# An RWKV-7 head stage reordered: four closing products of y on GpSimd, its per-head scales on ScalarE, a and b turned ahead of r and k

## The chip, the cores and the metric

One core of one Trainium2 chip runs the whole program. The metric is the device time of one execution in microseconds (us), smaller is better. The engines are named as in the profile: PE (TensorE), DVE (VectorE), ACT (ScalarE), POOL (GpSimd) and SP (SyncE, which here only issues transfers).

## What is computed

Two layers over 512 tokens of width 1024, each a token mixer and a feed-forward part with a normalisation behind either. Layer 0 mixes by a gated MLP, layer 1 by RWKV-7. The change lies in RWKV-7's part that works head by head (16 heads of 64):

```python
kk = (k * k_k); kk = kk / maximum(sqrt(sum(kk * kk, per head)), 1e-12)
k = k * (1.0 + (a - 1.0) * k_a)
# per token: sa = -S kk;  S = S * decay + sa b^T + v k^T;  y = S r      with b = kk * a
y = (y - mean) * rsqrt(var + GN_EPS) * gn_g + gn_b        # mean and var per head
bonus = sum(r * k * r_k, per head) * v
out = ((y + bonus) * g) @ w_o
```

## The kernel before

The dense products (projections, feed-forward, output) stream weight slabs of 512 KB and fill most of the span. Between the last projection and the output product `rw_out` lies the head stage. It has eight steps: step i is token block i // 2 (128 tokens) and half i % 2 of the heads (8 heads, 512 columns). The recurrence over 128 tokens is not run token by token: PE forms the interactions of the decayed vectors a, b, k, r (`gram`), the triangular system is inverted from blocks of 8 up to 64 (`grown`, `inverse`), and products then give y and the new state.

A loop of eight iterations carries several steps at once, written out by hand for every engine: in iteration q the engines prepare step n = q + 1, invert step q, run the products of step s = q - 1 (state, x, u, y) and close step `before` = q - 2. Each engine works in the order in which its code stands. There is no scheduler; semaphores alone tie the engines together. What each does in an iteration, in order:

- DVE: `spread_rows` (rows of the small blocks), the variance of y of `before`, kk and its norm, `decay_before`, `invert_blocks` (14 short dependent operations), the normalising of kk, `scale_b` and `decay_ab` (the vectors b and a), `grow` 0, `decay_kr` (k and r), `sum_bonus`, `grow` 1, `centre_y`, `pass_state` and last `mask_grams`, eight copies of the interactions out of PSUM under a mask, L1222.
- POOL: two masks (`level_of`), four products that scale k (`scale_k`, L478 to L483), two that form r * k * r_k (`bonus_terms`, L492, L495), six that close y (`finish`, L513 to L520), and four copies (`place_diagonal`, L466). All of these but the masks and copies are 128x512.
- ACT: copies out of PSUM, squares, square roots and exponentials; `copy_left` carries the left factor of each level of the inversion (L809), `copy_ub` (L804) the lower half of u.
- PE: `x_product` (L1635, L1638; it waits for the sixth masked copy of the step after), `log_decays` (L1540, L1542), `replicate` (L1580), `u_top`, `y_known`, `x_carry` (L1658), then the levels of the inversion (L1588) with `u_bottom`, `state_change` and `y_rest` (L1699) between them, the turning of the four vectors (L1554), and two halves of `interactions` (L1568).
- SP: reads of `early` (decay, a, k, r; 1 MB) and `late` (g, v; 0.5 MB) of a step from device memory, two buffers each, issued when the old contents are used.

`mask_grams` of iteration q writes what `spread_rows` of iteration q + 1 and `x_product` of the next iteration read, so it closes the ring. The waits of POOL that matter here:

```python
pool.wait_ge(bonus_ready, s.nth(1, 1))      # finish: the sums of step `before` on DVE
pool.wait_ge(yr_ready, s.nth(1, 1))         # finish: 1 / std of y on DVE
dve.wait_ge(rk_ready, n.nth(1, 1))          # sum_bonus: bonus_terms on POOL
```

Of the kernel before, what the change touches and what calls it, by code (L numbers as in the profile page):

```python
# [33 lines left out]
class Step:  # L34
# [9 lines left out]
    def loaded(self):  # L44

        return 16 * (self.t + 1)


def trunk(nc, x, ln1_g, ln1_b, ln2_g, ln2_b, ffn_w1, ffn_w2, gm_w_in, gm_vn_g, gm_vn_b, gm_ws, gm_bs,
# [42 lines left out]
    with ExitStack() as ctx:  # L92
# [47 lines left out]
        def over(name, shape):  # L140
            size = 4
            for n in shape[1:]:
# [36 lines left out]
        late = over("late", [P, 2, 2, HALF])  # L179
# [9 lines left out]
        xs, yc, y_square, rk, bonus_v = (over(name, [P, HALF]) for name in ("xs", "yc", "y_square", "rk", "bonus_v"))  # L189
# [13 lines left out]
        us = over("us", [P, HALF])  # L203
        cursor[0] = cursor[1] - TT * D * 4
        assert place["us"] + HALF * 4 <= cursor[0]
# [37 lines left out]
        early_in, late_in = [sem("early_in0"), sem("early_in1")], [sem("late_in0"), sem("late_in1")]  # L243
        late_used = sem("late_used")
        cum_summed, lx_ready, exp_ready = sem("cum_summed"), sem("lx_ready"), sem("exp_ready")
# [38 lines left out]
        def _(sp):  # L284
# [17 lines left out]
            def load_late(t, half):  # L302
                sp.dma_start(late[:, half, :, :],
                             proj[4:6, t, :, half * HALF:(half + 1) * HALF].rearrange("u p n -> p u n")
                             ).then_inc(late_in[half], 16)

            for name, _, count, source in stream:
                if count == KT:
                    for i in range(count // SLOTS):
                        for j in range(SLOTS):  # L310
# [4 lines left out]
                            if (name, i, j) == ("rw_out", 0, 1):  # L315
# [7 lines left out]
                                load_late(0, 0)  # L323
                                load_late(0, 1)
                                for step in range(2, STEPS + 1):
# [57 lines left out]
        def _(pool):  # L383
# [67 lines left out]
            def level_of(q, level):  # L451

                pool.wait_ge(diag_ready, q.nth(4, 4))
# [16 lines left out]
            def scale_k(n):  # L470
# [3 lines left out]
                def link(k, instruction):  # L474
                    instruction.then_inc(k_linked, 1)
                    pool.wait_ge(k_linked, n.nth(3, k))
# [1328 lines left out]
```

## Time and profile before

| | |
|---|---|
| time, median of 3 runs (lowest, highest) | 1456.98 us (1455.24, 1458.12) |
| the profiled execution: time, span | 1458.38 us, 1456.7 us |
| busy of the span: PE, DVE, ACT, POOL | 93%, 49%, 33%, 42% |
| mean granted clock of PE over the span | 0.942 |
| the chain that ended last: PE, DVE, ACT | 73%, 20%, 3% |
| one iteration of the head stage, q = 3 to 6 | 34.16 to 34.43 us |

The span is the time from the first to the last instruction; the execution's own time lies 1.7 us above it. Busy times overlap, so a share says what an engine did and not what held the end back. A granted clock of 1.00 is 2.4 GHz and 0.50 is 1.2 GHz.

### The profile page before, as it was taken

What the parts mean: (1) busy time and instruction counts of PE and PEld (TensorE: products, weight loads), DVE (VectorE), ACT (ScalarE), POOL (GpSimd) and SP (SyncE); (2) the same over time, 40 slices, a digit from 0 to 9 for tenths busy, and PEclk for the clock granted to TensorE, in tenths of its full rate; (3) what the DMA queues carried; (4) which work ended last, traced back from release to release, by engine and by line L of the source; (5) the groups of instructions that cost most, each with busy time, mean ns of one, the idle gap of its engine ahead of it and who ended that gap; (6) DMA issues with size and microseconds to landing.
All of it is one profiled execution on the core that took longest, in us unless ns stands there. A gap on an engine that the chain in (4) does not pass through costs nothing.

```text
span 1456.7 us, 22580 instructions
## 1 busy us (share of the span) xinstructions
PE 1352.2 (93%) x9097; PEld 1100.6 (76%) x9097; DVE 708.9 (49%) x894; ACT 474.1 (33%) x719; POOL 616.7 (42%) x377
## 2 busy tenths in 40 slices
PE   7989999999999979999958888889889999999996
PEld 6878888888888833577837877778678888888885
DVE  3476811113444583444666778884474111234447
ACT  4443232223322223343333333443232222332230
POOL 5334354444444520343533555554244444354441
PEclk9999999999999989999977788787899999999998
DMA  7223333333433222443421011101134333233321
GB/s 260 73 85 121 95 105 101 100 90 113 134 113 93 86 101 88 144 154 126 137 87 31 11 63 58 49 17 59 58 101 130 101 94 93 86 116 91 96 72 58
DMA packets 108972, 138.19 MB, mean 95 GB/s; under 512 B 6162, under 2 KB 81986, under 8 KB 108900
## 3 DMA queue, kind: packets, MB, share of 16 engines
q1 hardware_dynamic: 104292, 120.37, 27.3%
q10 hardware_dynamic: 4608, 16.78, 3.1%
q8 instruction: 55, 0.90, 0.3%
q14 instruction: 17, 0.14, 0.0%
HBM read 122.45 MB, written 14.68 MB: 94 GB/s over the span
## 4 chain that ended last, share of the span: by engine, by line
PE 73%; DVE 20%; ACT 3%; issue 2%; SPq 1%; DMA 1%; ACTq 0%; DVEq 0%
PE bank L1359 33%; PE bank L1411 8%; PE bank L1413 8%; PE bank L1412 8%; DVE a_lo L934 3%; PE bank L1504 2%; PE bank L1521 2%; PE bank L1699 2%; PE bank L1554 2%; PE bank L1568 2%; DVE x_tok L962 2%; DVE x_tok L960 1%; DVE gram L1222 1%; DVE stats L951 1%; PE bank L1588 1%
## 5 line engine op out<-in xcount | busy, mean ns | idle before, releaser
L390 POOL TENSOR_TENSOR w_lo<-raw,w_hi 128x1024 fp32r<-128x1024 f32 x184 | 455.0, 2479 | 649.6 <-ACT w_hi L561 637.2
L1359 PE MATMUL bank<-w_hi,a_hi 128*128 128x512 f32 x896 | 279.7, 393 | 17.3 <-DVE a_lo L934 11.9
L561 ACT ACTIVATE w_hi<-raw 128x1024 fp32r<-128x1024 f32 x184 | 193.6, 1056 | 291.7 <-PE bank L1359 279.8
L1359 PE MATMUL bank<-w_lo,a_hi 128*128 128x512 f32 x896 | 276.9, 390 | 0.0
L1359 PE MATMUL bank<-w_hi,a_lo 128*128 128x512 f32 x896 | 276.5, 390 | 0.0
L1411 PE MATMUL bank<-xT_hi,w_hi 128*128 128x512 f32 (+1 forms) x640 | 236.9, 370 | 0.0
L1412 PE MATMUL bank<-xT_lo,w_hi 128*128 128x512 f32 (+1 forms) x640 | 236.1, 369 | 0.0
L1413 PE MATMUL bank<-xT_hi,w_lo 128*128 128x512 f32 (+1 forms) x640 | 236.1, 369 | 0.0
L934 DVE TENSOR_TENSOR a_lo<-big,a_hi 128x512 fp32r<-128x512 f32 x64 | 140.7, 2203 | 182.6 <-ACT a_hi L580 179.5
L1359 PEld LDWEIGHTS bank<-w_hi,a_hi 128*128 128x128 f32 x896 | 166.2, 188 | 59.2 <-issue 17.4
L1359 PEld LDWEIGHTS bank<-w_lo,a_hi 128*128 128x128 f32 x896 | 168.8, 188 | 35.5
L1359 PEld LDWEIGHTS bank<-w_hi,a_lo 128*128 128x128 f32 x896 | 168.6, 188 | 35.5
L1043 DVE TENSOR_TENSOR big<-relu 128x512 f32 (+1 forms) x64 | 45.8, 716 | 275.9 <-ACT relu L688 275.9
L1413 PEld LDWEIGHTS bank<-xT_hi,w_lo 128*128 128x128 f32 x640 | 121.4, 190 | 20.1
L1412 PEld LDWEIGHTS bank<-xT_lo,w_hi 128*128 128x128 f32 x640 | 121.5, 190 | 19.9
L1411 PEld LDWEIGHTS bank<-xT_hi,w_hi 128*128 128x128 f32 x640 | 121.4, 190 | 19.8
L688 ACT ACTIVATE relu<-bank 128x512 f32<-128x512 f32 x64 | 38.4, 600 | 237.7 <-PE bank L1413 237.7
L934 DVE TENSOR_TENSOR a_lo<-mix,a_hi 128x512 fp32r<-128x512 f32 x24 | 43.1, 1796 | 83.4 <-ACT a_hi L736 83.4
L1222 DVE TENSOR_TENSOR gram<-bank,keep_before 128x512 f32<-128x512 f32 x64 | 39.8, 684 | 13.0 <-PE bank L1568 12.6
L1588 PE MATMUL bank<-grown_t,level_m 32*32 32x32 f32 x1024 | 15.1, 218 | 33.0 <-DVE grown_t L1266 19.4
L719 ACT ACTIVATE stage<-bank 128x512 f32<-128x512 f32 x48 | 26.0, 594 | 55.5 <-PE bank L1359 40.4
L1588 PEld LDWEIGHTS bank<-grown_t,level_m 32*32 32x32 f32 x1024 | 13.1, 130 | 36.7 <-DVE grown_t L1266 20.5
(210 smaller groups left out, 1498.3 us busy)
## 6 DMA issues: line engine op xcount, KB each, us to landing
raw<-in_ffn_w SPq DMA_DIRECT2D x128, 512.0 KB, 3.9
raw<-in_rw_w_rkv SPq DMA_DIRECT2D x24, 512.0 KB, 3.7
proj<-stage ACTq DMA_DIRECT2D x24, 512.0 KB, 2.7
raw<-in_gm_w_in SPq DMA_DIRECT2D x16, 512.0 KB, 4.1
early<-proj SPq DMA_DIRECT2D x8, 1024.0 KB, 7.5
raw<-in_gm_w_out SPq DMA_DIRECT2D x8, 512.0 KB, 3.5
raw<-in_rw_w_o SPq DMA_DIRECT2D x8, 512.0 KB, 3.6
late<-proj SPq DMA_DIRECT2D x8, 512.0 KB, 4.7
```

What stands on the lines that cost most here:

```text
L390: nc.gpsimd.tensor_tensor(w_lo[:, j, :], raw[:, j, :], w_hi[:, j, :].bitcast(F32), ALU.subtract).then_inc(w_lo_ready, 1)
L561: nc.scalar.activation(w_hi[:, j, :], raw[:, j, :], ACT.Copy).then_inc(w_hi_ready, 1)
L688: nc.scalar.activation(relu[:, j % 2, :], bank[j][:], ACT.Relu).then_inc(bank_read, 1)
L934: nc.vector.tensor_tensor(a_lo[:, j, :], source(i * SLOTS + j), a_hi[:, j, :].bitcast(F32), ALU.subtract).then_inc(a_lo_ready, 1)
L962: nc.vector.scalar_tensor_tensor(y, y, rstd[:, 0:1], gains[:, 1, :], ALU.mult, ALU.add).then_inc(result, 1)
L1043: nc.vector.tensor_tensor(big[:, i * SLOTS + j, :], relu[:, j % 2, :], relu[:, j % 2, :], ALU.mult).then_inc(squared, 1)
L1222: nc.vector.tensor_tensor(gram[:, n.half, h:h + 3:2, 2 * g:2 * g + 2, :], bank[GRAM[b]][:].rearrange("p (e a t) -> p e a t", e=2, a=2), ke ...
L1359: last = nc.tensor.matmul(bank[2 * t + h][:], a[:, j, tok], w[:, j, h * HALF:(h + 1) * HALF], start=start and a is a_hi and w is w_hi, sto ...
L1411: nc.tensor.matmul(dst, w_hi[:, j, col], xT_hi[:, k, tokens], start=k == 0, stop=False)
L1412: nc.tensor.matmul(dst, w_hi[:, j, col], xT_lo[:, k, tokens], start=False, stop=False)
L1413: last = nc.tensor.matmul(dst, w_lo[:, j, col], xT_hi[:, k, tokens], start=False, stop=k == KT - 1)
L1588: last = nc.tensor.matmul(out[quadrant(m), h * Q:(h + 1) * Q], a[quadrant(m), h, :], b[quadrant(m), h, :], start=True, stop=True)
```

## The change

POOL's `finish` loses its two products by head. ACT does them as eight multiplications of 128x64 each, one for a head, with a scale per partition: `scale_bonus` before `copy_ua`, `scale_y` after the second `copy_left`. POOL then closes y of step `before` after `scale_k` and ahead of `bonus_terms`. Scaling k takes three products in place of four, k * (a * k_a + (1 - k_a)), with 1 - k_a in `k_rest`, formed once. `yc` gets a second buffer and `late` a third. On DVE the block inversion stands ahead of the variance of y and of the norm of kk, `grow` 0 and 1 move ahead of `decay_ab` and `decay_kr` respectively, and `sum_bonus` moves behind `centre_y`. On PE `y_rest` changes places with `state_change`, and the turning is split: a and b after the second level, r and k between the two corner products, with both halves of `interactions` at the end. `level_of` on POOL waits for `spread_rows`.

The diff, cut to its core (the renaming of `yc[:]` and `late[:, half]` to the new buffers, the new semaphores and the new helpers' indentation are left out):

```diff
-        late = over("late", [P, 2, 2, HALF])
+        late = over("late", [P, 3, 2, HALF])
...
-        kkn, p_mid, p_inv, p_prev, scratch, k_gain = (over(name, [P, HALF]) for name in
-                                                  ("kkn", "p_mid", "p_inv", "p_prev", "scratch", "k_gain"))
+        kkn, scratch, k_gain = (over(name, [P, HALF]) for name in ("kkn", "scratch", "k_gain"))
...
+        us, p_mid, p_inv, p_prev = (over(name, [P, HALF]) for name in ("us", "p_mid", "p_inv", "p_prev"))
+        k_rest = over("k_rest", [P, D])
...
-                                load_late(0, 1)
-                                for step in range(2, STEPS + 1):
+                                for step in range(3):
+                                    load_late(step)
+                                for step in range(2, STEPS + 2):
                                     if step < STEPS:
                                         sp.wait_ge(tok_ready, 4 * (step - 1))
                                         sp.wait_ge(rk_ready, step - 1)
                                         load_early(step // 2, step % 2)
-                                    if step > 2:
-                                        sp.wait_ge(late_used, step - 2)
-                                        load_late((step - 1) // 2, (step - 1) % 2)
+                                    if step > 4:
+                                        sp.wait_ge(late_used, step - 4)
+                                        load_late(step - 2)
...
-                pool.wait_ge(diag_ready, q.nth(4, 4))
+                pool.wait_ge(spread_ready, q.nth(1, 1))
...
                 link(1, nc.gpsimd.tensor_tensor(k_gain[:], now[:, AA, :], gain, ALU.mult))
-                link(2, nc.gpsimd.tensor_tensor(k_gain[:], k_gain[:], gain, ALU.subtract))
-
+                if n.i == 0:
+
+                    link(2, nc.gpsimd.tensor_tensor(k_gain[:], k_gain[:], gain, ALU.subtract))
+                    pool.wait_ge(kk_scaled, n.nth(1, 1))
+                    link(3, nc.gpsimd.tensor_tensor(k_gain[:], k_gain[:], now[:, KK, :], ALU.mult))
+                    nc.gpsimd.tensor_tensor(now[:, KK, :], now[:, KK, :], k_gain[:], ALU.add).then_inc(k_ready, 1)
+                    return
+                pool.wait_ge(zeroed, 1)
+                link(2, nc.gpsimd.tensor_tensor(k_gain[:], k_gain[:], k_rest[:, n.half * HALF:(n.half + 1) * HALF],
+                                                ALU.add))
                 pool.wait_ge(kk_scaled, n.nth(1, 1))
-                link(3, nc.gpsimd.tensor_tensor(k_gain[:], k_gain[:], now[:, KK, :], ALU.mult))
-                nc.gpsimd.tensor_tensor(now[:, KK, :], now[:, KK, :], k_gain[:], ALU.add).then_inc(k_ready, 1)
+                nc.gpsimd.tensor_tensor(now[:, KK, :], now[:, KK, :], k_gain[:], ALU.mult).then_inc(k_ready, 1)
...
+                pool.wait_ge(rk_ready, n.nth(1, 1))
...
-                half, col = s.half, slice(s.half * HALF, (s.half + 1) * HALF)
...
-                pool.wait_ge(late_in[half], s.loaded())
-
-                pool.wait_ge(bonus_ready, s.nth(1, 1))
-                link(1, nc.gpsimd.tensor_tensor(heads(bonus_v[:]), heads(late[:, half, VV, :]),
-                                                per_head(BONUS + s.i % 4), ALU.mult))
-                pool.wait_ge(yr_ready, s.nth(1, 1))
-                link(2, nc.gpsimd.tensor_tensor(heads(yc[:]), heads(yc[:]), per_head(YR), ALU.mult))
-                link(3, nc.gpsimd.tensor_tensor(yc[:], yc[:], gn[:, 0, col], ALU.mult))
-                link(4, nc.gpsimd.tensor_tensor(yc[:], yc[:], gn[:, 1, col], ALU.add))
-                link(5, nc.gpsimd.tensor_tensor(yc[:], yc[:], bonus_v[:], ALU.add))
-                nc.gpsimd.tensor_tensor(y_tok[:, s.t, col], yc[:], late[:, half, GG, :], ALU.mult
+                    pool.wait_ge(pool_linked, s.nth(3, k))
+                pool.wait_ge(y_scaled, s.nth(1, 1))
+                link(1, nc.gpsimd.tensor_tensor(now, now, gn[:, 0, col], ALU.mult))
+                link(2, nc.gpsimd.tensor_tensor(now, now, gn[:, 1, col], ALU.add))
+                pool.wait_ge(bonus_scaled, s.nth(1, 1))
+                link(3, nc.gpsimd.tensor_tensor(now, now, bonus_v[:], ALU.add))
+                pool.wait_ge(late_in[s.i % 3], s.loaded_late())
+                nc.gpsimd.tensor_tensor(y_tok[:, s.t, col], now, late[:, s.i % 3, GG, :], ALU.mult
                                         ).then_inc(late_used, 1)
                 pool.wait_ge(late_used, s.nth(1, 1))
...
                 if n:
                     scale_k(n)
-                    bonus_terms(n)
                 if before:
                     finish(before)
+                if n:
+                    bonus_terms(n)
                 place_diagonal(q)
...
+            def scale_y(s):
+                act.wait_ge(yr_ready, s.nth(1, 1))
+                for h in range(HH):
+                    now = of_head(yc[:, s.i % 2, :], h)
+                    last = nc.scalar.activation(now, now, ACT.Copy, scale=small[:, YR, h:h + 1])
+                last.then_inc(y_scaled, 1)
+
+            def scale_bonus(s):
+                act.wait_ge(late_in[s.i % 3], s.loaded_late())
+                act.wait_ge(bonus_ready, s.nth(1, 1))
+                if s.i:
+                    act.wait_ge(late_used, s.i)
+                for h in range(HH):
+                    last = nc.scalar.activation(of_head(bonus_v, h), of_head(late[:, s.i % 3, VV, :], h), ACT.Copy,
+                                                scale=small[:, BONUS + s.i % 4, h:h + 1])
+                last.then_inc(bonus_scaled, 1)
...
-                if before:
-                    std_y(before)
                 if n:
                     square_kk(n)
+                if before:
+                    scale_bonus(before)
                 if s:
                     copy_ua(s)
                 if n:
                     decays_of(n)
-                    norm_of(n)
                 if s:
                     copy_xb(s)
                 copy_left(q, 0)
+                if before:
+                    std_y(before)
+                if n:
+                    norm_of(n)
                 if s:
                     copy_ub(s)
                 copy_left(q, 1)
+                if before:
+                    scale_y(before)
+                copy_left(q, 2)
                 if n:
                     turned_pairs(n)
-                copy_left(q, 2)
+                copy_corner(q)
                 if s:
                     square_y(s)
-                copy_corner(q)
...
+            scale_bonus(Step(STEPS - 2))
+            scale_y(Step(STEPS - 2))
...
-                if s.i:
-                    dve.wait_ge(late_used, s.i)
-                nc.vector.tensor_tensor(by_head(yc[:]), by_head(bank[Y_BANK][:]), per_head(YSUM), ALU.subtract
+                if s.i >= 2:
+                    dve.wait_ge(late_used, s.i - 1)
+                nc.vector.tensor_tensor(by_head(yc[:, s.i % 2, :]), by_head(bank[Y_BANK][:]), per_head(YSUM), ALU.subtract
...
+                if s.i:
+                    dve.wait_ge(y_scaled, s.i)
...
+                if n:
+                    scale_kk(n)
+                    decay_before(n)
+                invert_blocks(q)
+                if n:
+                    sum_kk(n)
                 if before:
                     variance_y(before)
+                grow(q, 0)
                 if n:
-                    scale_kk(n)
-                    sum_kk(n)
+                    normalise_kk(n)
                 if before:
                     rstd_y(before)
                 if n:
-                    decay_before(n)
-                invert_blocks(q)
-                if n:
-                    normalise_kk(n)
                     scale_b(n)
                     decay_ab(n)
-                grow(q, 0)
+                grow(q, 1)
                 if n:
                     decay_kr(n)
-                    sum_bonus(n)
-                grow(q, 1)
                 if s:
                     centre_y(s)
+                if n:
+                    sum_bonus(n)
+                if s:
                     pass_state(s)
                 if n:
                     mask_grams(n)
...
+            then(nc.vector.tensor_scalar(k_rest[:], k_a[:], -1.0, 1.0, ALU.mult, ALU.add))
             nc.vector.memset(start[:], 0.0).then_inc(zeroed, 1)
...
-            dve.wait_ge(late_used, STEPS - 1)
...
+            dve.wait_ge(late_used, STEPS - 1)
...
+            def turn_ab(n):
+
+                pe.wait_ge(tok_ready, n.nth(4, 2))
+                for p in range(PAIRS):
+                    c = slice(p * P, (p + 1) * P)
+                    for a, source in ((A_, tok_ar[:, A_, c]), (B_, tok_bk[:, n.i % 3, 0, c])):
+                        nc.tensor.transpose(bank[GRAM[p]][:, a * P:(a + 1) * P], source, ident[:])
+
+            def turn_rk(n):
+
                 pe.wait_ge(tok_ready, n.nth(4, 4))
                 for p in range(PAIRS):
                     c = slice(p * P, (p + 1) * P)
-                    for a, source in enumerate((tok_ar[:, A_, c], tok_ar[:, R_, c],
-                                                tok_bk[:, n.i % 3, 0, c], tok_bk[:, n.i % 3, 1, c])):
+                    for a, source in ((R_, tok_ar[:, R_, c]), (K_, tok_bk[:, n.i % 3, 1, c])):
                         last = nc.tensor.transpose(bank[GRAM[p]][:, a * P:(a + 1) * P], source, ident[:])
                     last.then_inc(turned_summed, 1)
...
                 if s:
-                    state_change(s)
+                    y_rest(s)
                 level_left(q, 1)
                 if s:
-                    y_rest(s)
+                    state_change(s)
                 level_right(q, 1)
                 if n:
-                    turn_tokens(n)
+                    turn_ab(n)
                 corner_left(q)
                 if n:
-                    interactions(n, 0)
+                    turn_rk(n)
                 corner_right(q)
                 if n:
+                    interactions(n, 0)
                     interactions(n, 1)
...
-            turn_tokens(Step(0))
+            turn_ab(Step(0))
+            turn_rk(Step(0))
```

`loaded_late()` is `16 * (self.i // 3 + 1)`; the buffer of a step is `s.i % 3` for `late` and `s.i % 2` for `yc`.

## Rows read from the trace of the kernel before

**Rows 1.** Windows: us, busy (count) of five engines, PE's clock, DMA share, GB/s.
```profile
752.97:782.85 29.88, 20.23 (x389) 15.56 (x389) 20.87 (x45) 9.73 (x20) 11.35 (x14) 0.60 0.13 37
...
815.71:850.44 34.73, 31.08 (x527) 27.56 (x526) 28.47 (x56) 14.10 (x27) 19.66 (x19) 0.75 0.14 47
...
884.87:919.15 34.28, 28.40 (x526) 25.08 (x525) 28.25 (x55) 13.98 (x27) 19.65 (x19) 0.85 0.17 48
```

**Rows 2.** Timeline of DVE, q = 4: start, length, instruction, count.
```profile
885.98 1.69 DVE L1234 TENSOR_TENSOR spread<-block_n,select 128x512 f32<-128x512 f32 x1
...
896.41 1.37 DVE L1135 TENSOR_TENSOR kkn<-kkn,small 128x512 f32<-128x512 f32 x1
...
901.04 1.74 DVE L1150 TENSOR_TENSOR tok_bk<-scratch,p_inv 128x512 f32<-128x512 f32 x1
...
904.99 0.67 DVE L1165 TENSOR_REDUCE small<-rk 128x8 f32<-128x512 f32 x1
...
912.12 0.87 DVE L1180 TENSOR_TENSOR start<-bank,start 64x256 f32<-64x256 f32 x2
...
914.20 5.04 DVE L1222 TENSOR_TENSOR gram<-bank,keep_before 128x512 f32<-128x512 f32 x8 [0.31 <-PE bank L1568]
```

**Rows 3.** Timeline of DVE with POOL quiet, and the clearing of `start`.
```profile
741.48 0.91 DVE L1305 MEMSET start<- 128x1024 f32 x1 [0.28 <-DVE inverse L1304]
...
764.11 0.69 DVE L1135 TENSOR_TENSOR kkn<-kkn,small 128x512 f32<-128x512 f32 x1
...
784.43 1.00 DVE L1234 TENSOR_TENSOR spread<-block_n,select 128x512 f32<-128x512 f32 x1
```

**Rows 4.** Timeline of PE around and in q = 4.
```profile
883.90 0.46 PE L1635 MATMUL bank<-start,turned 128*128 128x128 f32 x2 [0.32 <-DVE gram L1222]
...
886.60 1.08 PE L1540 MATMUL bank<-early,cumulate 128*128 128x512 f32 x2
...
888.33 1.10 PE L1580 MATMUL bank<-spread,keep_block 128*128 128x512 f32 x2
...
893.25 1.14 PE L1658 MATMUL bank<-us,gram 64*64 64x64 f32 x16
...
895.74 0.75 PE L1588 MATMUL bank<-grown_t,level_m 32*32 32x32 f32 x64 [1.35 <-DVE grown_t L1257]
...
904.66 3.67 PE L1699 MATMUL bank<-us,gram 128*128 128x64 f32 x16
```

**Rows 5.** Windows around PE's idle time in q = 4.
```profile
899.45:901.80 2.35, 0.00 (x0) 0.00 (x0) 2.31 (x3) 0.00 (x0) 2.27 (x2) 0.96 0.00 0
...
903.66:911.60 7.94, 7.94 (x155) 7.70 (x156) 4.08 (x8) 1.30 (x3) 1.29 (x4) 0.50 0.69 202
```

**Rows 6.** Timeline of PE at the end of the stage.
```profile
1008.79 0.80 PE L1635 MATMUL bank<-start,turned 128*128 128x128 f32 x2
...
1013.97 1.91 PE L1745 MATMUL bank<-ident,y_tok 128*128 128x128 f32 x8
...
1026.88 2.00 PE L1699 MATMUL bank<-us,gram 128*128 128x64 f32 x16 [0.68 <-ACT us L804]
```

**Rows 7.** Timeline of POOL in q = 4, and in q = 7.
```profile
893.67 1.26 POOL L495 TENSOR_TENSOR rk<-rk,r_k 128x512 f32<-128x512 f32 x1
...
896.19 1.04 POOL L516 TENSOR_TENSOR yc<-yc,small 128x512 f32<-128x512 f32 x1
...
992.66 1.27 POOL L517 TENSOR_TENSOR yc<-yc,gn 128x512 f32<-128x512 f32 x1
```

**Rows 8.** Timeline of ACT in q = 4.
```profile
891.15 1.28 ACT L772 ACT_TABLE_LOAD   x1
892.44 0.18 ACT L772 ACTIVATE decays<-bank 128x8 f32<-128x8 f32 x1
...
897.61 0.59 ACT L804 ACTIVATE us<-bank 64x512 f32<-64x512 f32 x1 [0.68 <-PE bank L1666]
...
904.80 0.38 ACT L809 ACTIVATE left<-bank 128x256 f32<-128x256 f32 x1 [6.61 <-PE bank L1588]
```

More of the change, by code:

```diff
@@ L202, in trunk @@
         spread = over("spread", [P, BASE, HH, BASE])
-        us = over("us", [P, HALF])
+        us, p_mid, p_inv, p_prev = (over(name, [P, HALF]) for name in ("us", "p_mid", "p_inv", "p_prev"))
+        k_rest = over("k_rest", [P, D])
+        assert cursor[0] <= cursor[1] - TT * D * 4
         cursor[0] = cursor[1] - TT * D * 4
-        assert place["us"] + HALF * 4 <= cursor[0]
         y_tok = over("y_tok", [P, TT, D])
@@ L300, in load_early, with load_late @@
                              ).then_inc(early_in[half], 16)
-            def load_late(t, half):
-                sp.dma_start(late[:, half, :, :],
+            def load_late(step):
+                t, half = step // 2, step % 2
+                sp.dma_start(late[:, step % 3, :, :],
                              proj[4:6, t, :, half * HALF:(half + 1) * HALF].rearrange("u p n -> p u n")
-                             ).then_inc(late_in[half], 16)
+                             ).then_inc(late_in[step % 3], 16)
             for name, _, count, source in stream:
@@ L1328, in _ @@
             dve.wait_ge(gn_in, 32)
-            then(nc.vector.tensor_tensor(by_head(bonus_v[:]), by_head(late[:, half, VV, :]), per_head(BONUS + last_step.i % 4),
+            dve.wait_ge(late_used, STEPS - 1)
+            then(nc.vector.tensor_tensor(by_head(bonus_v[:]), by_head(late[:, last_step.i % 3, VV, :]), per_head(BONUS + last_step.i % 4),
                                          ALU.mult))
@@ L1335, in _ @@
             dve.wait_ge(yr_ready, STEPS)
[L1336 to L1340 removed]
+            then(nc.vector.tensor_tensor(by_head(yc[:, last_step.i % 2, :]), by_head(yc[:, last_step.i % 2, :]), per_head(YR), ALU.mult))
+            then(nc.vector.tensor_tensor(yc[:, last_step.i % 2, :], yc[:, last_step.i % 2, :], gn[:, 0, col], ALU.mult))
+            then(nc.vector.tensor_tensor(yc[:, last_step.i % 2, :], yc[:, last_step.i % 2, :], gn[:, 1, col], ALU.add))
+            then(nc.vector.tensor_tensor(yc[:, last_step.i % 2, :], yc[:, last_step.i % 2, :], bonus_v[:], ALU.add))
+            nc.vector.tensor_tensor(y_tok[:, TT - 1, col], yc[:, last_step.i % 2, :], late[:, last_step.i % 3, GG, :], ALU.mult).then_inc(late_used, 1)
             for k in range(2, KT):
@@ L1630, in x_product @@
                     pe.wait_ge(start_ready, 2 * (s.i - 1))
-                pe.wait_ge(late_in[s.half], s.loaded())
+                pe.wait_ge(late_in[s.i % 3], s.loaded_late())
                 if s.i + 1 < STEPS:
@@ L1638, in x_product @@
                         last = nc.tensor.matmul(head(bank[X_BANK], h), gram[:, s.half, h, K_A, :],
-                                                head(late[:, s.half, VV, :], h), start=False, stop=True,
+                                                head(late[:, s.i % 3, VV, :], h), start=False, stop=True,
                                                 skip_group_check=True)
@@ L1679, in state_change @@
                                      skip_group_check=True)
-                    last = nc.tensor.matmul(dst, head(tok_bk[:, s.i % 3, 1, :], h), head(late[:, s.half, VV, :], h),
+                    last = nc.tensor.matmul(dst, head(tok_bk[:, s.i % 3, 1, :], h), head(late[:, s.i % 3, VV, :], h),
                                             start=False, stop=True, skip_group_check=True)
@@ L1692, in y_known @@
                         nc.tensor.matmul(head(bank[Y_BANK], h), gram[:, s.half, h, K_R, :],
-                                         head(late[:, s.half, VV, :], h), start=False, stop=False,
+                                         head(late[:, s.i % 3, VV, :], h), start=False, stop=False,
                                          skip_group_check=True)
```

28 lines of the change are left out of this document (11 added, 17 removed).

## The prediction

> **What bounds the kernel now.** I read the page first, then the windows by iteration, then the timeline of each engine in one iteration. The diff touches the head stage, some 287 us in which POOL, ACT, DVE and PE pass eight steps of work along; the rest of the 1456.7 us span is dense products that it leaves alone. I call T the start of an iteration: the first DVE instruction after the eight masked copies `gram`. The windows run from T to T: 29.88 us for q = 0, 32.86 for q = 1 (between the bounds of its neighbours), 34.73 for q = 2, and 34.16 to 34.43 for q = 3 to 6, one of which stands [rows 1]. In all of them every engine has gaps, so it is the order of the work that bounds, not its amount.
>
> In q = 4 (T = 884.87) the path runs through DVE. `spread` takes 1.69 us where it took 1.00 with POOL quiet; the four products from 896.41 to 902.7 come 1.6 us apart where they came 0.7 apart with POOL quiet [rows 2, 3]. Only behind them does DVE reach the growth of the blocks, so PE gets its second level product at 903.66 and `y_rest` at 904.66 [rows 4]. PE stood idle from 899.45; within 2.35 us of idle its granted clock had begun to fall, and then it was 0.50, the lower level of 1.2 GHz, through 7.94 us of unbroken work [rows 5]. `y_rest` took 3.67 us there, against 2.00 at 2.4 GHz [rows 4, 6]. The masked copies begin at T + 29.33 and take 4.95 us in all [rows 2].
>
> **The change part by part.**
>
> *POOL.* Two closing products leave (the bonus by head, and y by its reciprocal, 1.04 us) and one of the four of k; they were off the path, and POOL's load falls by some 3.5 us. But the order is now: k, close y, bonus terms, place the diagonal; and closing y waits for `y_scaled` from ACT. Behind that wait in POOL's queue stand four closing products, two bonus terms and the placing; on DVE `sum_bonus` waits for the bonus terms, and `pass_state` and all the `gram` copies stand behind it. Before, the bonus terms ended at 894.93 [rows 7], ten microseconds ahead of `sum_bonus` at 904.99 [rows 2]. That slack is what the change spends.
>
> *DVE.* The `ab` products now run while POOL waits, so they should cost 0.7 each instead of 1.6: 3.8 us less on DVE. `variance_y`, `sum_kk` and `rstd_y` leave the front, so the inversion no longer waits for them.
>
> *ACT.* Sixteen scalings of 128x64 are new, eight ahead of `copy_ua`, eight after the second `copy_left`. No row has this shape. A 128x8 took 0.18 and a 128x256 0.38 [rows 8], on which line 64 columns take 0.23. The lower bound is 0.12 apart, overlapped as the 128x8 was with its successor (0.07 apart for 0.18): 1.0 us for eight. The upper is 0.38 each, 3.1 us for eight. I take 0.24 and 1.95, nearest to the line, for a scale read per partition can hardly be cheaper than a constant. The Trainium skill (ScalarE: Activation LUTs, What ACT_TABLE_LOAD costs) says that a pointer operand adds 93 ns and that neighbours overlap by 93 ns; by its figures eight take an estimated 1.9 us. No run so far shows it. The root of y now stands after the first `copy_left`, and its table load of 1.28 us [rows 8] lies ahead of `copy_ub`.
>
> **One iteration worked through**, in the times of q = 4, at full clock. `spread` ends at 886.91, 0.7 earlier. PE's own queue (start products, decays) holds `replicate` at 888.33 as before [rows 4]. The inversion starts at 889.45, when that has landed; its fourteen short operations and the two that build the blocks take 4.3 to 4.6 us, as before: over at 894.1. So the first level can start when `x_carry` ends, 894.35, against 895.74 [rows 4]. Two level products of 0.70 with `u_bottom` between (the shape of `x_carry`, 1.1) end at 896.9. ACT's row of `copy_left`, table load and two roots lasts until 897.1, `copy_ub` until 897.75 (before 898.2 [rows 8]). Then `y_rest` from 897.8 to 899.7, second level 900.4, `copy_left` 900.85, `scale_y` 902.9. The same `copy_left` ended at 905.2 before [rows 8]: the front has gained 4.3 us, of which `scale_y` takes 1.95 back.
>
> From there six products on POOL. Alone one takes 1.27 with 0.07 between [rows 7], 8.05 in all; some of them meet `decay_kr` on DVE, for which I put 0.65 (0 to 1.3): 911.65. Then `sum_bonus` 0.67 and `pass_state` 1.95 (0.17 and twice 0.87 with gaps [rows 2]): 914.27. The copies began at 914.20 before. The gain is gone: 34.35 us against 34.28, +0.1 (−1.7 to +1.8 with the bounds of the scalings and of the meetings).
>
> **The clock.** At full clock PE ends the first half of `interactions` near 910 and then has nothing until the first copy is there at 914.9: 5 us idle, twice what the fall took before [rows 5]. So the next iteration begins at 1.2 GHz, where those before began at 2.4. And there PE is now the path. `x_product`, 883.90 to 886.60, is 2.70 us; the same at half clock, 1008.79 to 1013.97, is 5.18 [rows 4, 6]; decays and `replicate`, of the same engine, I put at 1.2 more (0 to 2.6, all doubled): +3.7. When the light products around 895 let the clock fall ahead of `y_rest`, that costs 1.65 and the level product 0.35 more: +2.0. Before, 15 to 25% of the granted clock was missing in each of these iterations, 10 to 17 us at half rate [rows 1], so such a fall is nothing rare.
>
> **Sum.** *Start:* `k_rest` (128x1024) stands ahead of the clearing of `start`, for which PE waits. That clearing took 0.91 and had 0.28 before it [rows 3]: +1.2 (0.8 to 1.4). *q = 0 and 1* close no y, so nothing gates their `sum_bonus`. Their copies wait for PE's turns and interactions, which are now split by two corner products and by the wait for R; of the earlier inversion I count little more than the 0.7 of `spread`, 0.9 each: −1.8 (−6 to 0). *q = 2 to 6* at full clock: +0.1 each, −0.4 more for q = 2, which was longer: 0. *Cold starts* of q = 3 to 7: certain after a warm `y_rest`, less so after a cold one, as the idle then shrinks to 2 us; I count three of five, 3 × 3.7 = +11.1. *Cold `y_rest`* in two to three of five: +5. *q = 7* has no next step; its `replicate` comes 0.6 earlier: −0.5. Its two rows of scalings stand ahead of the last `copy_xa` on ACT, while PE turns finished rows of y: 0 (up to 2). The `late` loads have three buffers and wait for a `late_used` of one iteration earlier, so each has an iteration more: 0; without that cover a 0.5 MB load would show with the 5 us of its landing. Total +15; −1 for half-cold cases, +14. The profiled execution ran 1458.4 us, so 1472.4; it lay 1.4 above the median of the three runs, on whose scale that is 1471.
>
> The Trainium skill (TensorE: Matmul & The Clock Gate, What's actually happening) holds the ramp penalty under 1% of a typical span and warns against fitting counts of cold products; by that the clock terms would stay under an estimated 14.6 us instead of 16. No run so far shows which.
>
> **Rivals.**
>
> *Tie*, 0.14. PE's clock holds, or what is cold lies in its idle. The sum is then +1.2 − 1.8 + 0 − 0.5, about 1456 on the median's scale. For it: the mean granted clock differs between iterations of one pattern, 0.75 and 0.85 [rows 1], so the fall has no fixed place. Against: 5 us of idle is twice what a fall took.
>
> *Faster*, 0.15. `sum_bonus` finds its terms ready. The point from which it decides: six POOL products must end when PE has the first interactions, about T + 23, so `scale_y` must end by T + 15. An iteration would be 29 us, −26 in all, 1431. `scale_y` stands behind the `copy_left` that ends at T + 16, so this full form has 0.03. The smaller form has scalings at the lower bound and no meetings, −1.6 an iteration, and one cold start: 1451, 0.12.
>
> *Heavier*, 0.21. Once cold at T the chain is one thread and nothing absorbs it; five cold starts with `u_top` too (4.5 each) and five cold `y_rest`, +22 + 10 − 2: 1487.
>
> *Forecast*, 0.50, with its own range 1463 to 1480.
>
> A fifth of a per cent, 2.9 us, is about what a measurement of this kernel can tell from no change. Under 1454.1 lies 0.15, between that and 1459.9 0.13 (the tie, but for a tail), above 0.72. The range 1452 to 1486 takes in the tie and part of the smaller gain and leaves out the full gain and the larger half of the heavier case, under 2 in 10.
>
> **What the profile after would show.** Right, if: POOL idles some 9 us before its first closing product, and DVE idles until POOL's `rk`; `y_rest` starts near T + 13; the `ab` products take 0.7 us; the `gram` copies start at T + 29 or later; the granted clock is 0.50 at T. Wrong, if: the copies start before T + 27; a scaling takes over 0.35 or under 0.15; the clock is 1.00 throughout `x_product`; the inversion starts later than T + 4.6 at full clock.

## The result, and the profile after

The changed kernel takes 1489.95 us (median of 4, 1489.64 to 1491.87) against 1457.55 us for the kernel before on the same chip (median of 4, 1455.24 to 1458.39): a ratio of 1.0222, 95% interval 1.0209 to 1.0235. The forecast was 1471 with a range to 1486. The sign was right, the size was not. The ratios here and below leave out executions over 1.5% above the fastest of the same kernel: one of experiment 2 (1474.66 us), four of experiment 7 (1458.46 us and more), and one of the kernel before (2247.09 us, at a mean granted clock of 0.55 in place of 0.94).

First the page of the profile after: busy time of the engines, the granted clock in 40 slices (37 us each), and the chain that ended last.

```profile
PE 1385.6 (93%) x9097; PEld 1125.8 (76%) x9097; DVE 688.3 (46%) x895; ACT 498.1 (33%) x831; POOL 589.3 (40%) x356
...
PEclk9999999999999989999979758595799999999998
...
PE 75%; DVE 15%; ACT 4%; POOL 3%; issue 1%; SPq 1%; DMA 1%; ACTq 0%; POOLq 0%; DVEq 0%
```

Three dips to 5 with recoveries between them lie in the head stage. The windows from T to T, q = 0 to 6 in order, answer to [rows 1], with the same columns:

```profile
756.10:781.39 25.29, 18.27 (x389) 14.27 (x389) 18.41 (x45) 9.22 (x20) 10.52 (x11) 0.73 0.15 43
781.39:813.57 32.18, 28.89 (x527) 24.68 (x525) 22.76 (x53) 13.54 (x26) 10.34 (x11) 0.89 0.12 35
813.57:848.63 35.06, 28.59 (x522) 24.27 (x520) 25.04 (x56) 17.44 (x43) 15.31 (x15) 0.87 0.16 47
848.63:895.52 46.89, 42.86 (x531) 37.43 (x530) 25.28 (x55) 17.59 (x43) 15.32 (x15) 0.59 0.12 35
895.52:930.61 35.09, 28.63 (x522) 24.28 (x520) 25.06 (x56) 17.45 (x43) 15.33 (x15) 0.87 0.16 47
930.61:977.50 46.89, 42.83 (x532) 37.45 (x531) 25.24 (x56) 17.59 (x43) 15.32 (x15) 0.59 0.04 13
977.50:1012.55 35.05, 28.56 (x522) 24.13 (x520) 25.06 (x56) 17.45 (x43) 15.32 (x15) 0.87 0.06 18
```

Iterations alternate: 35.1 us, then 46.9 us at a granted clock of 0.59. In the long ones PE is busy 42.86 of 46.89 us: it is the bound there. The span grew by 33.4 us, and the windows account for it. The head stage starts 3.1 us later (756.10 against 752.97 [rows 1]); q = 0 gives 4.6 back and q = 1 0.7; q = 2, 4 and 6 cost 0.3, 0.8 and 0.9; q = 3 costs 12.5 and q = 5 12.7; from the last T to the end of the last `y_rest` it is 49.7 us in place of 41.3, 8.4 more. The 33.4 us are thus small terms that cancel (−0.1) and three parts that run at the low clock (12.46 + 12.66 + 8.37 = 33.5).

DVE in the iteration q = 4 (T = 895.52) answers to [rows 2]:

```profile
908.84 0.69 DVE L1168 TENSOR_TENSOR kkn<-kkn,small 128x512 f32<-128x512 f32 x1
...
910.97 0.69 DVE L1183 TENSOR_TENSOR tok_bk<-scratch,p_inv 128x512 f32<-128x512 f32 x1
...
915.28 1.75 DVE L1191 TENSOR_TENSOR tok_ar<-early,p_mid 128x512 f32<-128x512 f32 x1
...
922.23 0.69 DVE L1198 TENSOR_REDUCE small<-rk 128x8 f32<-128x512 f32 x1 [3.32 <-POOL rk L509]
...
924.84 2.48 DVE L1257 TENSOR_TENSOR gram<-bank,keep_before 128x512 f32<-128x512 f32 x4
```

ACT and POOL there, answering to [rows 7, 8]:

```profile
911.46 2.01 ACT L839 ACTIVATE yc<-yc,small 128x64 f32<-128x64 f32 x8
```

```profile
913.55 1.26 POOL L520 TENSOR_TENSOR yc<-yc,gn 128x512 f32<-128x512 f32 x1 [10.44 <-ACT yc L839]
...
919.58 1.27 POOL L506 TENSOR_TENSOR rk<-early 128x512 f32<-128x512 f32 x1
920.93 1.27 POOL L509 TENSOR_TENSOR rk<-rk,r_k 128x512 f32<-128x512 f32 x1
```

The four `ab` products take 0.64 to 0.69 us, and the front of the iteration is early. Then POOL, which has waited 10.44 us for ACT's eight scalings, closes y before it forms the bonus terms; `sum_bonus` waits 3.32 us for them, and the masked copies begin at T + 29.3, where they began before.

PE, from q = 4 into q = 5, answers to [rows 4]:

```profile
908.46 2.00 PE L1744 MATMUL bank<-us,gram 128*128 128x64 f32 x16 [0.89 <-ACT us L810]
...
913.96 0.59 PE L1656 MATMUL bank<-grown_t,gram 32*32 32x32 f32 x25
...
919.15 3.09 PE L1613 MATMUL bank<-turned 64*128 64x256 f32 x16
925.58 4.37 PE L1613 MATMUL bank<-turned 64*128 64x256 f32 x16 [3.34 <-DVE gram L1257]
...
935.06 2.02 PE L1579 MATMUL bank<-early,cumulate 128*128 128x512 f32 x2
...
953.43 3.67 PE L1744 MATMUL bank<-us,gram 128*128 128x64 f32 x16
...
962.67 0.69 PE L1656 MATMUL bank<-grown_t,gram 32*32 32x32 f32 x32
```

Windows over the same stretch, answering to [rows 5]:

```profile
918.00:921.70 3.70, 3.70 (x48) 3.04 (x48) 0.88 (x2) 2.85 (x7) 3.47 (x4) 0.54 0.00 0
921.70:924.90 3.20, 0.54 (x6) 0.14 (x2) 2.54 (x7) 0.00 (x0) 2.07 (x5) 0.99 0.47 104
924.90:962.80 37.90, 37.22 (x444) 32.71 (x446) 18.30 (x44) 13.77 (x35) 7.67 (x7) 0.51 0.10 34
```

PE stands idle for 3.3 us while DVE waits for POOL. The clock falls to 1.2 GHz behind that idle time and stays there for 37.9 us in which PE is busy 37.22. It comes back only while PE turns a and b of the next step, by T + 32. The first window shows a shorter fall: at 0.54, behind 1.96 us of idle time ahead of the turning of r and k, and over by the wait for the copies (0.99). Experiments 5 and 6 tell the two apart.

### The profile page after: what moved, and what is told of

Read it like the earlier page. It is cut to its first block, busy times and chain, and to the rows that moved or that the text cites. A ratio compares the mean times of both kernels' runs of the same rounds, so it can differ in the third digit from the quotient of the medians.

```text
span 1490.1 us, 22694 instructions
## 1 busy us (share of the span) xinstructions
PE 1385.6 (93%) x9097; PEld 1125.8 (76%) x9097; DVE 688.3 (46%) x895; ACT 498.1 (33%) x831; POOL 589.3 (40%) x356
## 4 chain that ended last, share of the span: by engine, by line
PE 75%; DVE 15%; ACT 4%; POOL 3%; issue 1%; SPq 1%; DMA 1%; ACTq 0%; POOLq 0%; DVEq 0%
PE bank L1398 32%; PE bank L1450 8%; PE bank L1452 8%; PE bank L1451 8%; DVE a_lo L967 3%; PE bank L1543 2%; PE bank L1560 2%; DVE x_tok L995 2%; PE bank L1613 2%; PE bank L1744 2%; DVE x_tok L993 1%; DVE stats L984 1%; PE bank L1633 1%; DVE x_tok L1010 1%; DVE gram L1257 1%
## 5 line engine op out<-in xcount | busy, mean ns | idle before, releaser
L1613 PE MATMUL bank<-turned 64*128 64x256 f32 x256 | 50.8, 517 | 14.9 <-DVE gram L1257 14.9
L1613 PEld LDWEIGHTS bank<-turned 64*128 64x128 f32 x256 | 38.2, 260 | 24.0 <-DVE gram L1257 19.7
L520 POOL TENSOR_TENSOR yc<-yc,gn 128x512 f32<-128x512 f32 x7 | 8.9, 1266 | 101.7 <-ACT yc L839 101.7
```

The lines of the kernel that those rows point to most:

```text
L1613: last = nc.tensor.matmul(bank[GRAM[b]][:, p % 2 * 2 * P:(p % 2 + 1) * 2 * P], turned4[r, n.half, p, (B_, K_)[g], :], turned4[r, n.half, p ...
```

## The experiments

Theory A: POOL's order gates the copies, PE's idle time ahead of them brings the low clock, and the low clock is the loss. Theory B, the rival: the new order on PE and ACT is slow in itself.

**1. The bonus terms ahead of the closing products.** POOL's gate goes; all else of the change stays.

```diff
+                if n: bonus_terms(n)      # POOL, iteration q
                 if before:
                     finish(before)
-                if n: bonus_terms(n)
```

> The changed kernel with one thing undone: POOL forms the bonus terms of the next step ahead of closing y. Theory A (the gate: sum_bonus on DVE waits for POOL, the gram copies wait behind it, PE idles, its clock falls for a whole iteration): the copies start at about T + 26, as soon as the first interactions are there, an iteration takes about 31 us in place of 35.05, and the iterations of 46.9 us vanish with the idle time; 1490 - 5 x 4 - 35 = 1435, up to 1455 if the 2 us of PE idle before the turning of r and k are enough for a fall. Theory B (the new order on PE and ACT is a slower thread by itself: split turning, table load ahead of the copy of u, sixteen scalings): the gate hides it, and little is won, 1480 to 1490.

Measured: 1444.46 us (1443.96 to 1445.09), ratio to the kernel before 0.991 (0.9892 to 0.9928). No iteration is over 34.21 us. B is out: with the new order on PE and ACT kept, the change gains about 13 us once POOL doesn't gate it, and the two calls in the wrong order cost 45 us. The clock still falls in this run, at `y_rest` and the turning of r and k (0.80 to 0.90 in the closing iterations), so they take 32.4 to 34.2 us and not the 31 expected.

**2. PE's idle time filled, the gate left.** Products of no use, 128x512, into a free bank: two ahead of the turning of r and k, three behind the first half of `interactions`.

```diff
                 if n and before:
+                    fill(n, 2)            # ahead of turn_rk
...
                     interactions(n, 0)
+                    if before: fill(n, 3)
```

> The changed kernel with work for nobody on PE: two products of 128x512 into the unused cumulation bank ahead of the turning of r and k, three behind the first half of the interactions, in the iterations that close a y. Nothing else moves, so the gate stays. Theory A with the clock as its larger part: the granted clock stays at 1.00 over the start of each iteration, all iterations take 35 to 37 us, none 46.9; 1490 - 12 - 12 - 9 = 1457, some 3 more for products that come too late. If the 46.9 us come from anything else than the idle time (a wait on a buffer, a transfer), they stay and the time is 1490 to 1500.

Measured: 1450.09 us (median of 5, 1446.96 to 1474.66; ratio 0.9937, 0.9917 to 0.9957). One of the windows of the profiled execution (1455.92 us), q = 4:

```profile
879.27:913.37 34.10, 30.67 (x536) 23.62 (x535) 24.85 (x55) 17.46 (x43) 15.33 (x15) 1.00 0.16 49
```

This run divides the loss. The gate is whole (`sum_bonus` still waits 3.32 us for POOL), five useless products were added to each iteration, and the kernel is 40 us faster than the changed one: at a clock of 1.00 all closing iterations take 34.10 to 34.12 us. The gate alone only uses up the gain; the clock makes the loss. The fill is not complete: PE still waits 2.00 us for the copies in q = 4, without a fall behind it, and in the last block of the profiled execution the clock is at 0.50 for 37.5 us all the same (998.0 to 1035.5, in half-microsecond windows), so that 1450 us is not yet the kernel at full clock.

**3 and 4. Two other ways round the gate.** The third puts `sum_bonus` behind the masked copies on DVE, the fourth the scalings of y ahead of the second `copy_left` on ACT.

```diff
-                if n: sum_bonus(n)        # 3, DVE
                 ...
                 mask_grams
+                if n: sum_bonus(n)
```

```diff
+                if before: scale_y(before)    # 4, ACT
                 copy_left(q, 1)
-                if before: scale_y(before)
```

> The changed kernel with sum_bonus behind the gram copies on DVE; POOL keeps its order (close y, then bonus terms). Theory A: the same cure as ahead of POOL, from the other side, since only DVE's place in the queue makes the copies wait: 1430 to 1450, within 8 of the run with the bonus terms first. A rival within A, that POOL's closing products hurt by taking turns with DVE rather than by the wait: then this run stays near 1485 while the bonus terms first help. Theory B: 1480 to 1490.

> The changed kernel with scale_y ahead of the second copy_left on ACT, so y_scaled comes when 1/std is there (about 1.7 us earlier in an iteration at full clock); the second copy_left comes 0.5 us later. Theory A: the gram copies start 1.7 us earlier, 33.4 us an iteration at full clock, PE's idle before them shrinks from 3.3 to 1.6 us; if that keeps the clock up in all iterations, 1450, if not, 1480. Theory B: 1490 or 2 to 3 more.

Measured: 1445.97 us for the third (median of 10, 1438.46 to 1456.49; ratio 0.992, 0.9893 to 0.9947), iterations of 31.8 to 33.2 us in an execution of 1438.8 us. It lies within 2 us of the first, so the rival within A is out too. The fourth took 1447.43 us (0.9927, 0.9905 to 0.995), with iterations of 34.15 us at a clock of 0.80, where 33.4 were expected. In the fourth, PE's fall comes earlier, at `y_rest` and the turning of r and k; PE has then no idle time between the halves of `interactions`, and the next iteration begins at full clock.

**5 and 6. Which idle time does it?** The fill of the second experiment split: only the two products ahead of r and k (5), only the three ahead of the copies (6).

> The changed kernel with only the two idle-time products ahead of the turning of r and k; the idle time before the gram copies stays, and grows, as PE comes to it at full clock. If the fall in that idle time is what the next iteration pays for, the iterations of 46.9 us stay or get more: 1485 to 1500. If the first fall (2 us of idle before the turning) is what starts it, this run comes near the one with all five products, 1450 to 1455.

> The changed kernel with only the three products behind the first half of the interactions, in the idle time before the gram copies. If that idle time is the one that counts, no iteration of 46.9 us is left, 34.1 to 36 us each: 1450 to 1458. If the fall before the turning of r and k is the one: 1485 or more.

Measured: 1489.24 us for the fifth (ratio 1.0203, 1.0171 to 1.0236), with iterations of 46.77 and 46.80 us as in the changed kernel; 1456.54 for the sixth (0.999, 0.997 to 1.001), none over 37.2. PE in the fifth, the second half of `interactions` with its wait, and the decays that follow:

```profile
923.19 4.37 PE L1618 MATMUL bank<-turned 64*128 64x256 f32 x16 [3.43 <-DVE gram L1257]
...
932.66 2.02 PE L1579 MATMUL bank<-early,cumulate 128*128 128x512 f32 x2
```

So the long falls of the changed kernel start in the 3.3 to 3.4 us ahead of the copies, the idle time that POOL's gate opens: filled, no closing iteration has one, and the other idle time alone costs some 6 us (1456.54 against 1450.09). The length of that idle time doesn't decide by itself how long a fall lasts. Behind 2.52 us of it in experiment 3 (q = 4) the second half of `interactions` ran at the low clock (4.05 us), and 3.5 us after the fall the clock was back; experiment 10 has a longer case.

**7, 8 and 11. Gate away and idle time filled.** The seventh joins the first experiment with one product ahead of `y_rest` and two ahead of the turning of r and k. The eighth has those two, and in place of the one ACT's `copy_ub` ahead of the table load for the root of y. The eleventh adds to the eighth one product ahead of the second half of `interactions`.

```diff
+                if s: copy_ub(s)          # 8 and 11, ACT: ahead of
                 if before: std_y(before)  # the table load
                 if n: norm_of(n)
-                if s: copy_ub(s)
```

> Bonus terms ahead of closing y (no gate), and PE kept busy where it idled in that run: one product ahead of y_rest, two ahead of the turning of r and k. Theory A: granted clock 1.00 through the closing iterations, copies start at T + 26 and an iteration takes 31 us in place of 32.4 to 34.2: 1444 - 5 x 2.3 - 3 = 1430. If the low clock in that run lies off the path: 1444.

> As the run before but without the product ahead of y_rest: instead ACT copies u's lower half ahead of the table load and the two roots, so y_rest starts 1.5 us earlier and PE's idle of 1.2 us there goes. The normalising of kk comes later (0.6 us), off the path. Expected 1 us an iteration under the run with the extra product: 1425; if the roots then hold DVE's products of a and b on the path: 1430 to 1435.

> The eighth experiment's kernel with one more product of no use in TensorE's remaining 1.3 us of idle time, ahead of the second half of the interactions. If what separates its 1428 us executions from its 1445 us ones is a fall of the clock behind that idle time, this one gives 1428 to 1431 us in nearly every execution. If the fall starts elsewhere, its times stay spread from 1428 to 1448 with a median near 1445.

Measured: the seventh's times go from 1436.76 to 1459.95 us (10 executions, median 1454.43), the eighth's from 1428.18 to 1447.93 (median 1445.56), the eleventh's from 1429.09 to 1434.37 (median 1433.57, ratio 0.9826, 0.9807 to 0.9846). The fastest executions lie 3 to 7 us above what was expected of the seventh (1430) and the eighth (1425), the medians 20 and more; the iterations at a clock of 1.00 take the 31.04 and 30.1 us expected. In the profiled execution of the seventh (1446.17 us) a single fall behind 1.33 us of idle made one iteration 42.64 us among others of 31.04 to 31.35:

```profile
897.34 2.07 PE L1618 MATMUL bank<-turned 64*128 64x256 f32 x16
900.74 3.70 PE L1618 MATMUL bank<-turned 64*128 64x256 f32 x16 [1.33 <-DVE gram L1257]
...
922.12 1.97 PE L1708 MATMUL bank<-us,gram 64*64 64x64 f32 x16
```

With that idle time cut to 0.27 us, in the eleventh, the spread of 20 us becomes one of 5; two of its five executions lie in the 1428 to 1431 us expected, the others 3 us above. What picks an execution of the seventh or eighth for the fall isn't settled.

**9 and 12. Are the scalings better on ACT?** The first and the eleventh experiment with the two products by head back on POOL, six closing products there.

```diff
+                nc.gpsimd.tensor_tensor(heads(bonus_v[:]), heads(late[...]), per_head(BONUS + ...), ALU.mult)
+                nc.gpsimd.tensor_tensor(heads(now), heads(now), per_head(YR), ALU.mult)
-                scale_bonus(before) ... scale_y(before)    # ACT
```

> The bonus terms stay ahead of the closing products, as in the first experiment, but the two by-head scalings of the closing values go back from ACT to POOL: six closing products on POOL, none on ACT. If the move to ACT is worth nothing once the bonus terms come first (POOL has nothing else to do then), closing iterations take 32 to 34 us and the whole 1444 to 1447, as the first experiment's did. If the two products hold POOL back (the next block's closing values or the next bonus terms late), iterations take 34 to 36 us and the whole 1450 to 1460. If moving the scalings off ACT lets the transposed copies go earlier there, iterations fall below 32 us and the whole below 1442.

> The eleventh experiment's kernel (bonus terms first, the idle time of TensorE filled) with the by-head scalings back on POOL as in the ninth. At full clock throughout, the eleventh's iterations take 30.1 us, the ninth's 30.6. If ACT's scalings are off the path once the clock is out of play, this one gives 30.1 us per iteration and 1428 to 1434, the same as the eleventh. If the products on POOL, which hold DVE up while both are at work (tok_ar at 1.41 in place of 0.69 us), cost time, it is 0.7 to 1.5 us per iteration slower, 1434 to 1442.

Measured: 1436.62 us for the ninth (ratio 0.9844, 0.9822 to 0.9866), 7.8 less than the first. That is the number of the expectation's third branch, below 1442, but not its reason: ACT still waits 1.68 us for PE ahead of the transposed copies in q = 4. The twelfth took 1435.92 us (0.9862, 0.9839 to 0.9885), 2.3 more than the eleventh; the two intervals overlap, and the profiled executions, each the fastest of its kernel, lie 6.1 us apart (1435.22 and 1429.09). Windows of one closing iteration each, first the ninth, then the twelfth, then the eleventh:

```profile
875.11:905.71 30.60, 27.09 (x527) 22.73 (x525) 27.23 (x55) 13.64 (x27) 18.51 (x17) 0.94 0.18 54
```

```profile
843.27:874.63 31.36, 28.88 (x532) 22.96 (x531) 27.35 (x55) 13.63 (x27) 18.49 (x17) 1.00 0.15 52
```

```profile
871.34:901.44 30.10, 28.82 (x533) 22.78 (x531) 25.65 (x55) 17.48 (x43) 15.72 (x15) 1.00 0.18 55
```

At a clock of 1.00 in both, ACT's scalings save 1.26 us an iteration: in the twelfth POOL's six products meet the `ab` products on DVE, and `tok_bk` takes 1.75 us where the eleventh has 0.69. That holds for the eleventh's order, with ACT's `copy_ub` ahead of the roots. The ninth lacks this and the fills, and takes 30.60 us, 0.50 more than the eleventh: its first `ab` product begins at T + 15.09, the twelfth's at T + 15.85, and these 0.76 us are as much as lies between 30.60 and 31.36. Yet without the fills the ninth beats the first. Both have 0.96 us of idle ahead of `y_rest`, and 1.05 to 2.17 (the ninth) and 1.38 to 1.55 (the first, q = 2 to 5) ahead of the turning of r and k; `y_rest` takes 2.00 us in the ninth's q = 4, 3.47 in the first's q = 5. Where the clock is about the same, each is ahead once: 32.06 us at 0.89 in the ninth against 32.67 at 0.90 in the first, but 33.04 at 0.85 against 32.43 at 0.84. So the difference seems to be where the clock falls (0.85 to 0.94 in the closing iterations against 0.80 to 0.90) more than the work; no run holds the clock of both. Why it falls later in the ninth stays open.

**10. Dense products at the start.** The changed kernel with four 128x256 products of no use ahead of `u_top`.

> The changed kernel with four 128x256 by 128x128 products of no use at the start of each closing iteration, between the replicate product and the running sums. If the low clock lasts through an iteration because TensorE has only small products there, these dense ones bring it back at the start: the two iterations of 46.9 us and the last block's end fall to about 40 to 42, iterations at full clock take 1.9 us more each (36 to 37), and the whole 1470 to 1480. If the clock stays low whatever TensorE runs, the slow iterations take 50 us, and the whole 1500 to 1510.

Measured: 1466.1 us (ratio 1.0056, 1.0037 to 1.0074), below both expectations, with five iterations of 37.1 to 37.8. It doesn't answer its question: the clock was back at 1.00 by the start of every iteration, so the four products never met a low clock, and whether they would lift one was not seen. But it shows something else. `y_rest` took 2.13 to 2.95 us, and PE waited 0.48, 2.00, 2.00, 4.78 and 4.78 us for the copies in q = 2 to 6. The last of q = 5:

```profile
955.86 4.38 PE L1617 MATMUL bank<-turned 64*128 64x256 f32 x16 [4.78 <-DVE gram L1257]
```

This wait is longer than the changed kernel's 3.34 us, and the clock did fall in it (0.50 from 953.5, in half-microsecond windows). It was back at 1.00 by 960.5, 7 us later, when the second half of `interactions` was done and `x_product` had begun; in the changed kernel the same 4.4 us of `interactions` at the low clock were followed by 32 us more of it. So the gate's idle time is where a long fall starts, and something else decides whether it becomes long. What that is stays open.

## Why the prediction was wrong

Step by step.

- *POOL's order as a gate, the gain exactly used up:* right. Forecast 34.35 us at full clock; 34.10 with the clock held (experiment 2). The copies begin at T + 29.3 (forecast T + 29.4), `y_rest` at T + 12.9 (T + 13), the inversion at T + 4.6, the `ab` products take 0.64 to 0.69 us (0.7), the eight scalings 2.01 us (1.95). The Trainium skill (ScalarE: Activation LUTs, What ACT_TABLE_LOAD costs) gave an estimated 1.9 for the eight; the trace agrees.
- *Gate gone, an iteration of 29 us:* the rival's number stands against 30.1 in experiments 8 and 11 at a clock of 1.00, and 32.4 to 34.2 with the clock left to itself (experiment 1).
- *PE idle and the clock low at T:* right in kind, for q = 3, 5 and 7; at T of q = 4 and 6 the clock was at 1.00. The idle time was 3.3 us, not 5, as the first half of `interactions` ended at T + 26.7 and not near T + 25.
- *The sizing of the low clock is the step that failed.* "Cold starts [...] three of five, 3 × 3.7 = +11.1" and "cold `y_rest` in two to three of five: +5" made 16 us. The count of three was right; the length was not. I let the low clock last through `x_product`, decays and `replicate`, and priced nothing behind them but `y_rest`, with the fall at `y_rest` a separate event. In fact one fall lasted until T + 32. Between a full-clock and a low-clock iteration (q = 4 and 5) the decays begin at T + 1.7 and T + 4.5, `y_rest` at T + 12.9 and T + 22.8, the first corner products (L1656, behind the turning of a and b) at T + 18.4 and T + 32.1: 2.7, 9.9 and 13.6 us late. Even the part that I did price was short: `replicate` ended 5.3 us late, not 3.7. The idle time then shrinks to 2.0 us, and the copies begin at T + 41.2, 11.9 late. So a low-clock iteration takes 11.8 us more than its neighbours; against the iterations of before, the two and the last block cost 33.5 us, where I had 16. In half-microsecond windows the three stretches at the low clock last 37.5, 37.5 and 48 us. Those of the kernel before last 10 to 17 us in its closing iterations, 23.5 in q = 0 and 20.5 near the end, so its trace allowed for somewhat more than I took, but not for 37.5.
- *Why every other one:* a low-clock iteration leaves PE 2.0 us of idle time ahead of the copies, the fall behind it lasts some 3.5 us, and the next iteration begins at full clock. I had seen that the idle shrinks to 2 us, but took it for "less so", not for a pattern.
- *Start:* `k_rest` cost 0.7 (forecast 1.2): 0.69 for itself and little around it. 2.8 more lie ahead of the change's code: the first `tok_ar` stands at 738.28 in place of 735.49; DVE's shorter wait for the first interactions (2.63 in place of 3.02) gives 0.4 back. The kernels of the experiments, with the same `k_rest`, have their first T at 752.5 to 754.5, the changed kernel at 756.10. So much of the 3.1 us is a difference between executions and not a cost of the change.
- *q = 0 and 1:* −4.6 and −0.7 where I counted −0.9 each; q = 0 was also at a clock of 0.73 in place of 0.60 [rows 1]. Inside the bounds that I gave.
- *A slip:* four `ab` products at 0.7 in place of 1.6 us are 3.6 us less, not 3.8; the trace has 3.55 (2.82 in place of 6.37 us for the four). The sum doesn't use it.
- *The heavier rival*, 1487, was nearest, but by another route: it had five cold starts of 4.5 us and five cold `y_rest`.

The rule of the Trainium skill that I set beside the clock's terms (TensorE: Matmul & The Clock Gate, What's actually happening), that the ramp costs under 1% of a span, doesn't hold here: what the low clock costs beyond the kernel before, 33.5 of 1490.1 us, is already 2.2%. By it I would have come out lower still.

## What to carry to other kernels

When a helper engine's order is changed, look for the consumer that waits behind a step the new order puts in front: here one swap of two calls on POOL turned a loss of 32 us into a gain of 13. When PE's path has idle time just ahead of its small products, price a fall of the clock over the longest low stretch that the trace before shows, not over the next two or three groups, and expect that it can last longer; then run the kernel once with the idle time filled by useless products, which separates most of the clock from the schedule in a single experiment. One such fall cost 11.6 us in experiment 7, so executions of one kernel can lie that far apart for it: look at the granted clock by windows before comparing medians.

The best kernel here is the eleventh, 1433.57 us (0.9826 of the kernel before), with three useless products in a closing iteration; without any it is the ninth, 1436.62 us (0.9844). Their intervals overlap, so the two are not told apart.

## What the runs showed of the hardware that was not expected

- The granted clock stayed at 1.2 GHz for 37.9 us with PE busy 37.22 of them, on products of 128x64, 64x64 and 32x32 for the most part; the two 128x512 decay products (2.02 us at the low clock) and the two of `replicate` in that stretch didn't bring it back. With 64x256 products in PE it did come back 7 us after a fall behind 4.78 us of idle (experiment 10).
- In both whole low-clock iterations of the changed kernel it came back while PE was turning 128x128 blocks (a turning took 0.42 us, then 0.27).
- A fall with nothing but 1.33 us of idle ahead of it cost 11.6 us (42.64 against 31.04 us, experiment 7); in others the same idle cost nothing (30.1 us at a clock of 1.00, experiment 8).
- Useless work on PE made the kernel faster by 40 us (1450.09 against 1489.95 us, experiment 2 against the changed kernel).
